# Two layers of a transformer block on one NeuronCore: rotary partners by copies, key factors per token, one-column products between the steps of a gate unit

## The reference, cut to what matters

```
proj = rms_norm(x, g) @ w_in          -> c_q 256, c_kv 128, k_rope 32, gq 512, gk 128, gv 128, pool 512, gates 3*1024
q = (rms_norm(c_q) @ w_uq)            # 8 heads of 96 = 64 plain + 32 rotary
k = [rms_norm(c_kv) @ w_ukv (64 per head), k_rope (32, the same for all heads)]
q, k = rms_norm over the 96 of a head, times a gain; the 32 rotary channels turned by (cos, sin)
gq (8 heads of 64), gk (2 heads of 64): rms_norm per head, gain, all 64 channels turned
turned = [x1*c - x2*s, x1*s + x2*c]   # x1, x2: the two halves of the rotary channels
attention without a mask; three branches (mla, gqa, pool), each times sigmoid(gate), summed, @ w_out
```

## Time and profile before

| | |
|---|---|
| median of three runs | 2081.68 us (2078.17 to 2084.25) |
| profiled execution: time | 2084.29 us |
| profiled execution: span | 2082.5 us |
| PE busy | 2008.6 us, 96% |
| DVE busy | 905.6 us, 43% |
| ACT busy | 641.4 us, 31% |
| POOL busy | 56.2 us, 3% |
| mean granted clock of TensorE | 0.989 of full speed |

### The profile page before, as it was taken

One profiled execution on the slowest core, in us unless ns is written; L12 is line 12 of the kernel. 1 busy time (PEld: TensorE's weight loads), 2 busy tenths in 40 slices (PEclk: granted clock), 3 DMA queues, 4 the chain that ended last, 5 costly groups with the idle time before them and its releaser, 6 DMA issues.

```text
span 2082.5 us, 31430 instructions
## 1 busy us (share of the span) xinstructions
PE 2008.6 (96%) x12446; PEld 1316.4 (63%) x12447; DVE 905.6 (43%) x1591; ACT 641.4 (31%) x972; POOL 56.2 (3%) x65
## 2 busy tenths in 40 slices
PE   8999999989999999999999999999999999999999
PEld 6864333423333333333333699889999999799999
DVE  3523221212221122112212557876885549776874
ACT  1422110101111111111111344544554344635553
POOL 0000000000000000000000220000000020000000
PEclk9999999999999999999999999999999999999999
DMA  9786999479999999999999544324564644235553
GB/s 347 287 327 283 415 425 418 163 300 427 427 425 425 427 427 426 426 425 428 425 419 425 175 152 142 122 85 158 163 209 135 185 132 142 82 122 162 189 186 112
DMA packets 186466, 580.51 MB, mean 279 GB/s; under 512 B 21472, under 2 KB 138976, under 8 KB 150400
## 3 DMA queue, kind: packets, MB, share of 16 engines
q1 hardware_dynamic: 186368, 579.08, 71.8%
HBM read 577.74 MB, written 1.31 MB: 278 GB/s over the span
## 4 chain that ended last, share of the span: by engine, by line
PE 73%; DMA 18%; DVE 4%; ACT 3%; issue 2%; SPq 0%; ACTq 0%; DVEq 0%
DMA ring<-in_w_gu 16%; PE bank L1108 16%; PE bank L1116 7%; PE bank L817 4%; PE bank L1398 4%; PE bank L1399 3%; PE bank L1400 3%; PE bank L1631 3%; PE bank L1633 3%; PE bank L1632 3%; PE bank L898 2%; PE bank L1054 2%; PE bank L1068 2%; PE bank L1647 2%; PE bank L1649 1%
## 5 line engine op out<-in xcount | busy, mean ns | idle before, releaser
L1108 PE MATMUL bank<-ring,heap 128*64 128x512 f32 x2112 | 476.1, 603 | 23.2 <-DMA ring<-in_w_gu 23.2
L1108 PEld LDWEIGHTS bank<-ring,heap 128*64 128x64 f32 x2112 | 147.0, 139 | 330.5 <-issue 283.0
L2285 DVE TENSOR_SCALAR heap<-bank 128x256 f32<-128x256 f32 x66 | 24.9, 419 | 676.9 <-PE bank L1108 676.9
L1116 PE MATMUL bank<-ring,heap 128*64 128x512 f32 x1056 | 235.2, 596 | 0.0
L1784 ACT ACT_TABLE_LOAD x32 | 41.1, 1283 | 500.8 <-DVE heap L2285 500.8
L1398 PE MATMUL bank<-h_hi,w_hi 128*128 128x256 f32 x640 | 186.1, 291 | 1.2 <-DVE w_lo L2417 1.2
L2612 DVE TENSOR_TENSOR w_lo<-ring,w_hi 128x2048 fp32r<-128x2048 f32 (+1 forms) x64 | 142.4, 2225 | 101.1 <-ACT w_hi L1990 101.1
L1631 PE MATMUL bank<-h_hi,w_hi 128*128 128x256 f32 x640 | 182.6, 285 | 3.4 <-DVE w_lo L2612 3.4
L1399 PE MATMUL bank<-h_lo,w_hi 128*128 128x256 f32 x640 | 183.1, 286 | 0.0
L1400 PE MATMUL bank<-h_hi,w_lo 128*128 128x256 f32 x640 | 183.0, 286 | 0.0
L1633 PE MATMUL bank<-h_hi,w_lo 128*128 128x256 f32 x640 | 182.1, 284 | 0.0
(11 more groups left out here) (369 smaller groups left out, 3021.0 us busy)
## 6 DMA issues: line engine op xcount, KB each, us to landing
ring<-in_w_gu SPq DMA_DIRECT2D x128, 2048.0 KB, 18.9
ring<-in_w_down SPq DMA_DIRECT2D x128, 1024.0 KB, 18.1
ring<-in_ffn_w_up SPq DMA_DIRECT2D x44, 1024.0 KB, 7.7
ring<-in_w_in SPq DMA_DIRECT2D x32, 1024.0 KB, 8.0
ring<-in_w_ada SPq DMA_DIRECT2D x24, 1024.0 KB, 11.4
ring<-in_ffn_w_down SPq DMA_DIRECT2D x16, 1024.0 KB, 5.1
ring<-in_w_out SPq DMA_DIRECT2D x8, 1024.0 KB, 5.0
ring<-in_w_in SPq DMA_DIRECT2D x3, 2048.0 KB, 27.3
```

Of the source, the lines that this page charges most:

```text
L1108: last = mm(psum[g][both[f], :], gu_input(xgT, k), wt[:, g, f, :], start=False, stop=k == DT - 1, skip_group_check=True)
L1116: last = mm(psum[bank][FEW * f:FEW * f + n, :], x[:, o:o + n], wt[:, 512 * f:512 * (f + 1)], start=k == 0, stop=k == DT - 1)
```

## The change: partners by DMA, key factors as columns turned to rows, sums of squares inside gate units

What the kernel does now in each of the two layers:

- **Partners by copies.** The permutation matrices are gone from the constants. `partners` issues DMAs on ACT's queue that copy partitions within SBUF: 2 for the shared key rows (16 partitions, 256 columns), 4 for the latent queries (16 partitions, 1024 columns), 8 for the grouped heads. All DVE work on them is then SBUF to SBUF, and for latent queries and keys only on the 32 rotary partitions.
- **Shared key rows turned once.** The 32 rotary channels of the latent keys are the same for all heads, so they are scaled and turned once (three DVE operations on 32x256) and then copied to the eight heads.
- **Key factors per token.** `ssgk` and `ssk` are made like those of the queries: tokens over partitions, 4 and 16 one- or two-column products. DVE and ACT work on 8 or 16 columns. `to_rows` then makes rows of them: a PE transpose of one column broadcast over 128 or 96 (4 transposes for `rgk` behind `done("gstd")`, 16 for `rk0` to `rk3` behind `done("kstd")`), and DVE multiplies the keys by these out of PSUM.
- **One product between two steps.** `by_unit` takes a function `beside` that is called before each of the 16 steps: `ssgq` and `ssgk` (12 products) stand in gates(0), `ssq` (16) in gates(2), `ssk` (16) in gates(3). gates(3) now stands ahead of `pl`, gates(4) behind it, and the `rk` transposes between gates(4) and gates(5).
- On ACT, the squares of the latent keys are two operations (32 and 64 partitions), both behind `full("ssq")` as the one was.

```diff
@@ -595,12 +589,12 @@
...
+        def partners(eng, pairs, half, first, last, done):
+
+            for dst, src in pairs:
+                for lo in range(first, last, 2 * half):
+                    for a, b in ((lo, lo + half), (lo + half, lo)):
+                        eng.dma_start(dst[a:a + half], src[b:b + half]).then_inc(done.sem, 16)
@@ -1388,28 +1382,30 @@
...
+                        if beside is not None:
+                            beside(cols // P * nk + k)
                         wh, wl = hi[:, k, cols:cols + P], lo[:, k, cols:cols + P]
                         mm(out, wh, x[0][:, k, :], start=k == 0, stop=False)
                         mm(out, wh, x[1][:, k, :], start=False, stop=False)
                         last = mm(out, wl, x[0][:, k, :], start=False, stop=k == nk - 1)
@@ -1453,19 +1449,39 @@
...
+                def by_query(b, slots, rows, sums, n, j):
+
+                    t, i = divmod(j, slots)
+                    o = NH * t + n * i
+                    last = mm(b[:, o:o + n], rows(i)[:, P * t:P * (t + 1)], sums, start=True, stop=True)
+                    if j == TT * slots - 1:
+                        last.then_inc(lay_full.sem, 1)
+                ssgq, ssgk = lay("ssgq"), lay("ssgk")
+                by_pair = const("pair").rearrange("p (a b) -> p a b", a=2)[:, :, 0]
+                def grouped_squares(j):
+                    if j < 8:
+                        by_query(ssgq, 4, lambda i: L["sq"][:, 3 + i, :], by_pair, 2, j)
+                    elif j < 12:
+                        by_query(ssgk, 2, lambda i: L["gates"][:, i, :], by_pair, 2, j - 8)
+                def latent_squares(name):
                     b = lay(name)
...
+                    return lambda j: by_query(b, NH, lambda i: L["sq"][0:MQ, i, :], const("ones", 1)[0:MQ, :], 1, j)
+                gates(0, grouped_squares)
+                def to_rows(bank, column, parts):
+                    for a in range(2):
+                        for t in range(TT):
+                            last = nc.tensor.transpose(bank[0:parts, T * a + P * t:T * a + P * (t + 1)],
+                                                       column(a, t).to_broadcast([P, parts]), ident)
                     last.then_inc(lay_full.sem, 1)
-                by_query("ssgq", 4, lambda i: L["sq"][:, 3 + i, :], const("pair").rearrange("p (a b) -> p a b", a=2)[:, :, 0])
-                squares("ssgk", const("pair"), L["gates"], [(0, 1), (1, 1)])
-                gates(0)
+                done("gstd")
+                to_rows(lay("rgk"), lambda a, t: L["rq"][:, 3, NH * t + 2 * a:NH * t + 2 * a + 1], P)
                 gates(1)
@@ -1486,18 +1502,9 @@
...
                 drained_act("uq3")
-                by_query("ssq", NH, lambda i: L["sq"][0:MQ, i, :], const("ones", 1)[0:MQ, :])
-                gates(2)
+                gates(2, latent_squares("ssq"))
                 done("ksq")
-                for i in range(4):
-                    squares(f"ssk{i}", const("ones")[0:MQ, 0:MQ], L["sq"], [(2 * i, 1), (2 * i + 1, 1)], MQ)
-                done("gn")
...
-                    tiles_of(lay(f"swg{i}"), const("swap_g"), L["gq"], 2 * i, P).then_inc(lay_full.sem, 1)
...
+                gates(3, latent_squares("ssk"))
...
-                for n in range(3, 7):
+                gates(4)
+                done("kstd")
+                for i in range(4):
+                    to_rows(lay(f"rk{i}"), lambda a, t: L["rq"][:, 2, NH * t + 2 * i + a:NH * t + 2 * i + a + 1], MQ)
+                for n in range(5, 8):
                     gates(n)
-                done("kn")
-                for i in range(4):
-                    tiles_of(lay(f"swk{i}"), const("swap_m")[0:MQ, 0:MQ], L["mk"], 2 * i, MQ).then_inc(lay_full.sem, 1)
-                gates(7)
@@ -1902,6 +1909,8 @@
...
+                ready("krope")
+                partners(act, [(kr_other, kr_own)], 16, HD, MQ, S["swapped_k"])
@@ -1914,31 +1923,36 @@
...
-                f(L["rs"][:, 6:8, :], L["rs"][:, 6:8, :], ACT.Sqrt).then_inc(S["gstd"].sem, 1)
+                f(rgk, rgk, ACT.Sqrt).then_inc(S["gstd"].sem, 1)
                 gates(0)
                 gates(1)
...
+                own("uq3")
+                partners(act, [(turned_at[n], L["mq"][:, 4 * n:4 * n + 4, :]) for n in range(2)], 16, 64, MQ, S["swapped_q"])
...
-                f(L["mk"][64:96, :, :], L["krope"][64:96, :].unsqueeze(1).to_broadcast([32, NH, T]), ACT.Copy) \
-                    .then_inc(S["krope"].sem, 1)
+                ready("rope_k")
+                f(L["mk"][64:96, :, :], kr_own[64:96, :].unsqueeze(1).to_broadcast([32, NH, T]), ACT.Copy) \
...
                 full("ssq")
-                ready("krope")
+                f(L["sq"][64:96, :, :], L["krope"][64:96, :].unsqueeze(1).to_broadcast([32, NH, T]), ACT.Square)
                 own("uk3")
-                f(L["sq"][0:MQ], L["mk"][0:MQ], ACT.Square).then_inc(S["ksq"].sem, 1)
+                f(L["sq"][0:HD], L["mk"][0:HD], ACT.Square).then_inc(S["ksq"].sem, 1)
+                out_dve("rgk")
+                partners(act, ((turned_g[0], L["gq"]), (turned_g[1], L["gk"])), HD // 2, 0, P, S["swapped_g"])
...
+                ready("kvar")
+                f(L["rq"][:, 2, :], L["rq"][:, 2, :], ACT.Sqrt).then_inc(S["kstd"].sem, 1)
                 gates(3)
                 gates(4)
-                ready("kvar", 2)
-                f(L["rs"][0:MQ], L["rs"][0:MQ], ACT.Sqrt).then_inc(S["kstd"].sem, 1)
@@ -2438,6 +2452,11 @@
...
+                v.tensor_scalar(kr_own[64:96, :], L["krope"][64:96, :], v2("k_head", 0)[64:96], None, ALU.mult) \
+                    .then_inc(S["krope"].sem, 1)
+                c.mark(v.tensor_copy(k_gain[0:HD, :], v2("k_head", 0)[0:HD]))
+                c.mark(v.memset(k_gain[64:96, :], 1.0))
@@ -2461,6 +2480,12 @@
...
+                ready("swapped_k", 2 * 16)
+                c.mark(v.tensor_tensor(kr_own[64:96, :], kr_own[64:96, :], const("cos_m")[64:96], ALU.mult))
+                c.mark(v.tensor_tensor(kr_other[64:96, :], kr_other[64:96, :], const("sin_m")[64:96], ALU.mult))
+                c.settle()
+                v.tensor_tensor(kr_own[64:96, :], kr_own[64:96, :], kr_other[64:96, :], ALU.add) \
+                    .then_inc(S["rope_k"].sem, 1)
@@ -2468,43 +2493,30 @@
...
-                v.reciprocal(L["rs"][:, 6:8, :], L["rs"][:, 6:8, :]).then_inc(S["gvar"].sem, 1)
+                v.reciprocal(rgk, rgk).then_inc(S["gvar"].sem, 1)
...
-                ready("gstd")
-                scaled(L["gk"], v2("gk_head", 0), L["rs"][:, 6:8, :]).then_inc(S["gn"].sem, 1)
+                taken(scaled(L["gk"], v2("gk_head", 0), two(full("rgk"))))
                 rest_early(6)
                 taken(mean(rq[:, 0, :], full("ssq")[:, 0:2 * NH], MQ))
                 own("ssq")
...
                 rest_early(7)
-                ready("gn")
-                for i in range(4):
-                    taken(mean(L["rs"][0:MQ, 2 * i:2 * i + 2, :], two(full(f"ssk{i}"))[0:MQ], MQ))
+                taken(mean(rq[:, 2, :], full("ssk")[:, 0:2 * NH], MQ))
+                own("ssk")
+                v.reciprocal(rq[:, 2, :], rq[:, 2, :]).then_inc(S["kvar"].sem, 1)
                 rest_early(8)
...
-                turned("q", turned_q)
-                v.reciprocal(L["rs"][0:MQ, 0:5, :], L["rs"][0:MQ, 0:5, :]).then_inc(S["kvar"].sem, 1)
-                rest_early(9)
-                v.reciprocal(L["rs"][0:MQ, 5:NH, :], L["rs"][0:MQ, 5:NH, :]).then_inc(S["kvar"].sem, 1)
-                rest_early(10)
@@ -2521,25 +2533,32 @@
...
-                ready("kstd")
...
+                ready("swapped_q", 4 * 16)
+                by_angle(const("cos_m")[rot], mq)
+                for n in range(2):
+                    by_angle(const("sin_m")[rot], turned_at[n][rot])
+                c.settle()
+                for n in range(2):
+                    part = mq[:, 4 * n:4 * n + 4, :]
+                    v.tensor_tensor(part, part, turned_at[n][rot], ALU.add).then_inc(S["rope_m"].sem, 1)
+                rest_early(9)
+                ready("krows")
+                for i in range(4):
+                    k = L["mk"][0:MQ, 2 * i:2 * i + 2, :]
+                    taken(scaled(k, k_gain[0:MQ, :], two(full(f"rk{i}"))[0:MQ]))
+                rest_early(10)
+                ready("swapped_g", 8 * 16)
+                for table, x in (("sin_g", turned_g[0]), ("sin_g", turned_g[1]), ("cos_g", L["gq"]), ("cos_g", L["gk"])):
+                    by_angle(const(table), x)
                 rest_early(11)
...
-                cos = const("cos_m")[0:MQ].unsqueeze(1).to_broadcast([MQ, NH, T])
+                c.mark(v.tensor_tensor(L["gq"], L["gq"], turned_g[0], ALU.add))
+                v.tensor_tensor(L["gk"], L["gk"], turned_g[1], ALU.add).then_inc(S["rope_g"].sem, 1)
                 rest_early(12)
-                c.mark(v.tensor_tensor(mk, mk, cos, ALU.mult))
-                c.settle()
-                own("swk3")
```

(29 more changed lines are left out.)

77 lines of the change are left out of this document (28 added, 49 removed).

## The result

| | before | after |
|---|---|---|
| median | 2079.93 us (4 runs) | 2109.34 us (4 runs, 2105.38 to 2114.06) |
| ratio, 95% interval | 1 | 1.0144 [1.0129, 1.0159] |
| profiled execution: time, span | 2084.29, 2082.5 us | 2105.38, 2103.6 us |
| mean granted clock | 0.989 | 0.982 |
| PE, DVE, ACT busy | 2008.6, 905.6, 641.4 us | 2007.4, 860.6, 636.1 us |

The forecast was 2108 us, in a range of 2086 to 2115, and it was 26.4 us more than before. By the medians it is 29.4 us more, so that 2109.34 lies only 1.3 us from the forecast is in part luck: the forecast stood on a median before of 2081.7, which is now 2079.93. The profiled execution is the quickest of the four. VectorE lost 45 us of work and the bounding engine next to none, since the products that remain run at the lower clock for longer (mean granted clock 0.982 for 0.989).

What follows compares the result with a forecast made beforehand. In the edited stretch TensorE's own instruction list bounds the kernel. Waits of 12.2 against 10.8 gained lose 1.4 us a layer; low clock adds 11.8: 13.2 a layer, 26.4 in both, on 2081.7 gives 2108 us, range 2086 to 2115.

Steps and rivals of the forecast that it cites:

- The shorter list: TensorE's instructions per layer: 22.8 us go, 12.0 come, so on the list alone 10.8 us gained a layer.
- two waits of 0.3: TensorE waits of gate units for a low part in the first layer, 0.3 us each, counted as gone.
- 0.21 us a product at full clock: Small products between gate steps pay both weight loads in full: 44 x 0.21 = 9.4 us a layer.
- The rival with hidden loads: Small products' loads hide behind the gate steps; with all hidden and the clock held, 2071 us; chance 0.07.
- the price of 0.05: Small product's cost in us from the skill's 60-cycle gap; with the clock held, about 2074 us.
- First wait: At `gstd`, behind gates(0), TensorE waits for the roots of the grouped keys before their transposes: 3.2 us.
- Second wait: At `ksq`, between gates(2) and gates(3), TensorE waits for the key squares, which need `ssq` complete: 3.6 us.
- Third and fourth: TensorE waits for low parts: unit 8, behind `ssk` sums, 0.7 us; unit 9, behind 16 transposes, 4.7 us.
- The clock low through gates(3): Behind the `ksq` wait the clock stays 0.50 through gates(3), 16.6 us long: 1.04 us a step, 7.5 us lost.
- All the low stretches: Low-clock losses per layer behind the three long waits, including gates(3) and `pl`: 1.9 + 7.5 + 0.9 + 1.5 = 11.8 us.
- the one behind the first wait: Low-clock loss in the dense work behind the `gstd` wait: 1.9 us, taken between 1.5 and 3.0.
- What the copies cost: The 14 copy issues on ScalarE, 0.38 us each, cost nothing on the path; late or dear copies, 2114 us, chance 0.06.

Runs made afterwards that it cites:

- e5: e3 with the low parts of units 7 and 8 on VectorE ahead of the sums of `ssq` and `ssk`; 2060.35 us, ratio 0.9901 to before.
- e1: The changed kernel with the latent key squares written early to the free tile `rs`, not waiting for `ssq`; 2104.31 us, ratio 1.0116 to before.
- e3: The changed kernel with key squares early, grouped-key transposes behind gates(1), and latent queries turned earlier on VectorE; 2084.21 us, ratio 1.0018 to before.
- e8: The changed kernel with the `ssk` products two at a time between steps 8 to 15 of gates(3); 2100.18 us, ratio 1.0096 to before.
- e9: e4 with the `ssk` products two at a time between steps 8 to 15 of gates(3); 2071.87 us, ratio 0.9968 to before.
- e4: The changed kernel with grouped-key transposes behind gates(1) and latent queries turned earlier on VectorE, key squares left late; 2082.80 us, ratio 1.0013 to before.
- e2: The changed kernel with the sixteen `ssk` products in one row behind gates(3); 2099.75 us, ratio 1.0102 to before.
- e7: The kernel before with `ssq` between the steps of gates(2), key squares in `rs`, unit 7's low part earlier; 2074.65 us, ratio 0.9971.

## Why the prediction was right

- **The shorter list, 10.8 us a layer.** Right. In e5 the part from `sslat` to the first scores takes 75.0 us in the first layer and 74.8 in the second, for 84.6 in both before:

```profile
1218.23 1.46 PE L811 MATMUL bank<-heap,consts_sb 128*128 128x256 f32 x6
...
1293.20 1.13 PE L1539 MATMUL bank<-heap 64*128 64x256 f32 x4
```

That is 9.7 and 9.9 us less, and 10.7 and 10.6 if e5's own waits there (1.0 and 0.7) are left out. Small errors of the sum cancel in this: it counts two waits of 0.3 as gone where one is, so 22.5 for 22.8; 44 products at the measured 0.22 are 9.7 for 9.4 (44 x 0.21 would be 9.2); and the 20 transposes take 2.1 us for 2.6 (16 of them 1274.09 to 1275.76). With these it is 22.5 - 11.8 = 10.7. That e5 is 21.6 us below before in the layers, exactly 2 x 10.8, is luck: 19.5 come from this part and some 2 from behind it, most of them the low stretch at 1458 us, which e5 doesn't have.
- **0.21 us a product at full clock, all of it paid.** Right: 0.57 to 0.58 a step less 3 x 0.12 is 0.22. The rival with hidden loads falls. So does the price of 0.05 that the prediction worked out from the Trainium skill, "TensorE: Matmul & The Clock Gate", section "Back-to-back issue gap" (60 cycles, about 25 ns, for 1 to 64 columns). The section itself says that its gap for a single product has no room for the weight load at few columns, and the trace agrees: 0.22 and not 0.05.
- **First wait, 3.2.** It was 4.0. The mis-sized term is the three operations on 32x256: I took 0.42 each from the earlier trace rows, and they take 2.2 us together (1224.26 to 1226.46); that is the 0.9. VectorE has no idle time between them, each is longer. The cause stays open: GpSimd is at work from 1219.46 on, and the low part behind them takes 2.60 us where the first of the layer took 2.29 with GpSimd idle, but no run separates this from the three standing right behind each other.

```profile
1224.26 0.61 DVE L2484 TENSOR_TENSOR heap<-heap,consts_sb 32x256 f32<-32x256 f32 x1
1224.79 0.85 DVE L2485 TENSOR_TENSOR heap<-heap,consts_sb 32x256 f32<-32x256 f32 x1
1225.68 0.74 DVE L2487 TENSOR_TENSOR heap<-heap 32x256 f32<-32x256 f32 x1
1226.46 2.60 DVE L2431 TENSOR_TENSOR w_lo<-ring,w_hi 128x2048 fp32r<-128x2048 f32 x1
```

- **Second wait, 3.6.** It was 3.5. But a second reason for it of 2.4 us, the low part of unit 7, was not in the prediction. It changed nothing in the forecast and everything in the first remedy, e1 and e3.
- **Third and fourth, 0.7 and 4.7.** 0 and 4.5 (4.6 in the second layer). The end of gates(3) and `pl` at the low clock cover the third. In e8 and e9 they run at full clock, with the low part of unit 8 still behind the sums of `ssk`, and the wait ahead of gates(4) is 0.5 us; in e9:

```profile
1275.63 0.39 PE L1394 MATMUL bank<-h_hi,w_hi 128*128 128x256 f32 x1 [0.51 <-DVE w_lo L2438]
```

e4 gives the fourth together with the first.
- **The clock low through gates(3), 16.6 us.** 17.2 and 16.6 in the two layers, with 1.06 a step for 1.04. e2 and e5 show the two conditions: with the wait but no products the clock is back inside the unit, after 3.4 or 6.8 us, with products but no wait it never falls. e3 against e5 is the closest pair: both have the same products in the same places, and the wait of 2.4 us or 0.3 ahead of them decides. Of a low step the three wide products take 0.64 us (3 x 0.213), so the small one takes 0.42 to 0.43, twice its price at full clock. The Trainium skill, "TensorE: Matmul & The Clock Gate", section "LDWEIGHTS (loading the stationary operand)", has one formula for a load, its columns over 1.2 in ns, with no split by clock; by it the small product would stay at 0.21, and the trace disagrees.
- **All the low stretches, 11.8 us a layer.** Right, and closer than its terms. Take the part from `sslat` to the first scores, without its waits (12.0 us in the first layer, 12.1 in the second, for 12.2): it is 13.2 and 10.7 us longer than in e5, 12.0 on average. Of the terms, the one behind the first wait, 1.9, was 2.5 and 1.3, since the low stretch there is 6.8 us long in one layer and 3.4 in the other.
- **What the copies cost.** Nothing on the path, as forecast, but an issue was dearer: eight take 5.0 us, 0.62 each for 0.38 from SP's queue in the earlier trace rows. They ran beside the squares, and ScalarE's next work came 1.24 us late, with TensorE waiting for neither:

```profile
1262.71 2.44 ACTq L597 DMA_DIRECT2D heap<-heap  x4
1264.62 1.91 ACT L1946 ACTIVATE heap<-heap 64x2048 f32<-64x2048 f32 x1
1265.18 2.54 ACTq L597 DMA_DIRECT2D heap<-heap  x4
1267.77 0.60 ACT L1872 ACTIVATE heap<-bank 128x512 f32<-128x512 f32 x1 [1.24 <-issue]
```

- **Not in the sum:** the low stretch at 1458 us is absent after, which gives about 1.7 us back in the first layer. The wait ahead of it is 1.8 us for 2.1; whether the change or chance took the stretch away is not shown (see the last section).

The sizes of the parts, from the layers: the first and fourth wait with their low stretches 24 us (after to e4); the second place with its low unit 23 us (e4 to e5); against them the shorter list, -22 us. 24 + 23 - 22 = 25, which is no check, since the three are differences of the same four numbers. Of those 22, about 6 come from `ssq` no longer standing in a row (e7), some 2 from behind the edited part, and the rest from the products that are gone.

## What to carry to other kernels

Moving small products between the steps of a dense unit takes away what used to cover the work of the other engines: list for each one who produces its operand and who waits for its result, since here all waits came from that and not from the products. A wait of some 3 us ahead of a stretch in which wide products alternate with small ones can cost two and a half to six times what it would bring ahead of plain dense work (17 or 20 us at half the clock against 3.4 to 6.8); if it can't be removed, start the small ones half a unit later (e9 gained 11.6 us over e4 by that alone). When a wait is removed, look in the same place for the next one behind it, before the result is held against the theory.

## What was not expected of the hardware

Whether a wait makes the clock fall isn't settled by its length alone. These are the waits ahead of the first product of the last part of the first layer and the clock behind them, in e3 and in e7; in the kernel before, 2.13 us had been enough.

```profile
1452.71 0.39 PE L1638 MATMUL bank<-h_hi,w_hi 128*128 128x256 f32 x1 [2.25 <-DVE w_lo L2624]
```

```profile
1453.00:1456.40 3.40, 3.40 (x30) 1.00 0.02 7
```

```profile
1451.07 0.47 PE L1642 MATMUL bank<-h_hi,w_hi 128*128 128x256 f32 x1 [2.49 <-DVE w_lo L2623]
```

```profile
1451.40:1454.80 3.40, 3.40 (x18) 0.52 0.00 0
```

2.25 us without a fall, 2.13 and 2.49 with one. What decides between them no run here shows. And low stretches far ahead of the edited code move one execution against another by 9 us, as much as several of the effects measured here: single executions are compared by the part that was edited.
